# Queries, keys, gate weights and the residual turned by VectorE and strided transfers instead of TensorE, with rotation and masks at other places, in a two-block float32 transformer kernel

## What is computed

```python
def first_block(x, ...):
    z_a, z_b, z_c, z_g = split(rms_norm(x, ln1_g) @ w_in)
    u, v = split(gelu(z_a)); v = layer_norm(v)
    y_a = (u * chunked_spatial_gating(v, sg_w, sg_b)) @ w_a_out   # tril(sg_w[g]), 8 groups of 128x128
    p, g = split(z_b); c = p * sigmoid(g)
    y_b = silu(layer_norm(depthwise_conv(c, 31 taps))) @ w_b_out
    q, k, vv = split(z_c)                                        # 8 heads of 64
    q = rms_norm(q per head); k = rms_norm(k per head)
    y_c = stick_breaking_attention(q, k, vv) @ w_c_out
    x = x + (gates[0] * y_a + gates[1] * y_b + gates[2] * y_c) @ w_out
    return x + (silu(gate) * val) @ w_down                       # up-projection and 3-tap convolution
def second_block(x, ...):
    u, g_rnn, q, k, v, g_attn, m_rnn, m_attn = split(rms_norm(x) @ w_in_2)
    y_rnn  = rg_lru(depthwise_conv(u, 4 taps)) * silu(g_rnn)
    y_attn = sliding_window_attention(rope(q), rope(k), v, sinks) * silu(g_attn)
    merged = sigmoid(m_rnn) * (y_rnn @ w_rnn_out_2) + sigmoid(m_attn) * (y_attn @ w_attn_out_2)
    return rms_norm(x + merged @ w_o_2)
```

## Time and profile before

| what | value |
|---|---|
| median of three runs | 1305.08 us |
| lowest, highest | 1303.37, 1305.54 us |
| profiled execution, its own time | 1305.04 us |
| span of its profile | 1303.3 us |
| TensorE busy | 1288.0 us |
| VectorE busy | 844.4 us |
| ScalarE busy | 601.7 us |
| GpSimd busy | 86.2 us |
| DMA, mean over the span | 103 GB/s |
| mean granted TensorE clock | 0.997 |

### The profile page before, as it was taken

The page is one execution under the profiler, slowest core; times in us unless marked ns, Lnnn a source line. Parts: engine busy times, 40 slices in busy tenths (PEclk is TensorE's granted clock), DMA queues, the critical chain, the costliest instruction groups (busy, mean ns, idle before and its releaser), DMA issues.

```text
span 1303.3 us, 15597 instructions
## 1 busy us (share of the span) xinstructions
PE 1288.0 (99%) x5951; PEld 1038.5 (80%) x5951; DVE 844.4 (65%) x1128; ACT 601.7 (46%) x878; POOL 86.2 (7%) x68
## 2 busy tenths in 40 slices
PE   9999999999999999999999999999999999999998
PEld 7888777788788888888888888887877777778886
DVE  6358899899867776666675335545467878544534
ACT  6234467332354443333343224412379899544233
POOL 0000222000000300000000002100012220000000
PEclk9999999999999999999999999999999999999999
DMA  8332211422322232322223222458322122224211
GB/s 296 139 98 64 66 66 65 161 85 83 124 68 95 98 97 97 97 97 97 97 97 97 97 97 93 166 161 200 119 79 73 65 81 69 94 65 162 97 65 64
DMA packets 121129, 134.48 MB, mean 103 GB/s; under 512 B 23752, under 2 KB 101488, under 8 KB 120560
## 3 DMA queue, kind: packets, MB, share of 16 engines
q1 hardware_dynamic: 121056, 133.70, 31.6%
q10 hardware_dynamic: 16, 0.00, 0.0%
HBM read 124.78 MB, written 8.91 MB: 103 GB/s over the span
## 4 chain that ended last, share of the span: by engine, by line
PE 93%; DVE 4%; ACT 1%; issue 1%; DMA 1%; SPq 0%; ACTq 0%; DVEq 0%
PE PS L1750 91%; PE PS L1817 2%; DVE WL L1069 1%; DMA XTOK<-in_x 1%; ACT WH L625 0%; DVE QK L1171 0%; DVE CACC L1224 0%; DVE RS L1265 0%; DVE MERG L1340 0%; DVE TMPY L1336 0%; DVE VATT L1153 0%; DVE VSG L1153 0%; ACT BT L712 0%; DVE Q L1533 0%; DVE UU L1239 0%
## 5 line engine op out<-in xcount | busy, mean ns | idle before, releaser
L625 ACT ACTIVATE WH<-STAGE 128x1024 fp32r<-128x1024 f32 x214 | 225.9, 1058 | 522.0 <-PE PS L1750 515.6
L1069 DVE TENSOR_TENSOR WL<-STAGE,WH 128x1024 fp32r<-128x1024 f32 x214 | 279.5, 1308 | 190.4 <-ACT WH L625 189.7
L1750 PE MATMUL PS<-XH,WH 128*128 128x512 f32 x960 | 381.8, 398 | 2.7 <-DVE YA L1565 2.7
L1750 PE MATMUL PS<-XH,WL 128*128 128x512 f32 x960 | 374.6, 390 | 0.0
L1750 PE MATMUL PS<-XL,WH 128*128 128x512 f32 x960 | 374.5, 390 | 0.0
L1750 PEld LDWEIGHTS PS<-XH,WH 128*128 128x128 f32 x960 | 180.7, 188 | 45.2 <-issue 4.0
L1750 PEld LDWEIGHTS PS<-XL,WH 128*128 128x128 f32 x960 | 180.6, 188 | 38.7 <-issue 2.4
L1750 PEld LDWEIGHTS PS<-XH,WL 128*128 128x128 f32 x960 | 180.6, 188 | 38.2
L1750 PE MATMUL PS<-WH,XH 128*128 128x512 f32 x224 | 87.9, 392 | 0.2 <-issue 0.2
L1750 PE MATMUL PS<-WH,XL 128*128 128x512 f32 x224 | 87.2, 389 | 0.0
L1750 PE MATMUL PS<-WL,XH 128*128 128x512 f32 x224 | 87.2, 389 | 0.0
(11 more groups left out here) (295 smaller groups left out, 1812.5 us busy)
## 6 DMA issues: line engine op xcount, KB each, us to landing
STAGE<-in_w_in SPq DMA_DIRECT2D x52, 1024.0 KB, 5.0
STAGE<-in_w_up SPq DMA_DIRECT2D x22, 1024.0 KB, 5.1
STAGE<-in_w_down SPq DMA_DIRECT2D x11, 1024.0 KB, 4.9
STAGE<-in_w_out SPq DMA_DIRECT2D x4, 1024.0 KB, 5.1
STAGE<-in_w_rnn_out SPq DMA_DIRECT2D x4, 1024.0 KB, 5.3
STAGE<-in_w_attn_out SPq DMA_DIRECT2D x4, 1024.0 KB, 5.1
STAGE<-in_w_o SPq DMA_DIRECT2D x4, 1024.0 KB, 5.0
XTOK<-in_x SPq DMA_DIRECT2D x4, 512.0 KB, 7.2
```

Of the source, the lines that this page charges most:

```text
L625: act.activation(ring(WH, n), staged(n), ACT.Copy).then_inc(hi_done, 1)
L1069: dve.tensor_tensor(ring(WL, n), staged(n), ring(WH, n).bitcast(F32), ALU.subtract)\
L1750: return pe.matmul(out_, lhsT, rhs, start=start, stop=stop, skip_group_check=True)
```

## The change

It touches five places. (1) The sums, the root and the scaling of queries and keys are done for each half by itself, directly behind its drains (iterations 8 and 10), and VectorE turns the tiles in 32x32 blocks in place; SyncE's queue stores them with four strided transfers, loads them as QKT, and ScalarE applies the gain in place. (2) The gate weights are loaded with their 32x32 blocks already exchanged (four transfers, later than before), turned and masked by VectorE. (3) The residual is turned in place by VectorE in units U_G + 10 and + 11 (loop indices; X1 is dead afterwards), stored in four strided transfers and loaded as XT2; XRES, its 32 turns and ScalarE's four copies go, and the two halves of the last product swap their PSUM banks. (4) Rotation, turns and drains of the second block are spread between the splits of units 8 to 13 of stage U_G, the keys' behind the first drain of U_GA. (5) Masks stand ahead of `lo`, the gating's norm starts ahead of stage U_B's drains, the convolution's norm moves one unit later, and the fourth turn of the input stands ahead of the wait for unit 1's weights.

```diff
+            def qk_store(i):
+                for a in range(4):
+                    sp.dma_start(QKROW[i].rearrange("(b j) (t a i) -> a j t b i", j=32, a=4, i=32)[a],
+                                 QK[32 * a:32 * a + 32, i].rearrange("p t (b i) -> p t b i", i=32))...
+            def qk_load(i):
+                sp.wait_ge(qk_out[i], 64)
+                sp.dma_start(QKT[:, i], QKROW[i].rearrange("(c p) s -> p c s", p=P))...
...
+                if p == U_B // 2 - 3:
+                    for a in range(4):
+                        sp.dma_start(SGW[32 * a:32 * a + 32]..., sg_w[0].rearrange("g (b i) (a j) -> a i g b j", i=32, j=32)[a])...
+                if p == U_B // 2:
+                    sp.wait_ge(qk_turned, TT)
+                    qk_store(0)
+                if p == U_B // 2 + 1:
+                    qk_load(0)
+                    sp.wait_ge(qk_turned, 2 * TT)
+                    qk_store(1)
+                if p == U_B // 2 + 2:
+                    qk_load(1)
...
                 if p == U_G // 2 + 7:
                     sp.wait_ge(q2_turned, TT)
                     q2_store(0)
+                    sp.wait_ge(x1_turned, KD)
+                    x1_store(0)
+                    x1_store(1)
                 if p == U_G // 2 + 8:
                     q2_load(0)
+                    x1_store(2)
+                    x1_store(3)
-                if p == U_G // 2 + 4:
-                    sp.wait_ge(drained, DR_G)
-                    sp.dma_start(XSCR, X1[:].rearrange("p k s -> p (k s)")).then_inc(x1_out, 16)
-                if p == U_H // 2 + 12:
-                    sp.dma_start(XRES[:].rearrange("p k s -> p (k s)"), XSCR).then_inc(x1_in, 16)
+                if p == U_H // 2 + 15:
+                    sp.wait_ge(x1_out, 64)
+                    sp.wait_ge(unit_done, U_H + 24)
+                    sp.dma_start(XT2[:], XROW.rearrange("(t p) d -> p t d", p=P)).then_inc(xt2_in, 16)
...
             act.wait_ge(vec_ready, 3)
-            qkt_copies(0)
-            act.wait_ge(vg_var, 1)
-            act.activation(SMALL[...], SMALL[...], ACT.Sqrt).then_inc(vg_sd, 1)
+            qkt_scaled(0)
...
-            for t in range(TT):
-                act.wait_ge(x2t_t, t + 1)
-                act.activation(XT2[:, t, :], PS[...], ACT.Copy).then_inc(x2t_ready, 1)
...
+            gate_norm(0)
             for i in range(12):
                 dve.tensor_tensor(dst, PS[:, i % 2, :], RBC[:], ALU.mult).then_inc(drained, 1)
...
-                lo(U_B + i + 4)
                 if 2 <= i < 13:
                     pair_mask(i - 1)
+                lo(U_B + i + 4)
...
-                if p == 1:
+                if p == 2:
                     dve.wait_ge(c_mean, 1)
...
+                if j == 0:
+                    lo(U_G + 8)
+                    q2_rope(0)
+                    lo(U_G + 9)
+                    q2_turn(0)
+                    lo(U_G + 10)
+                    x1_turn((0, 1, 2, 3))
+                    lo(U_G + 11)
+                    x1_turn((4, 5, 6, 7))
+                if j == 1:
+                    lo(U_G + 12)
+                    q2_rope(1)
+                    lo(U_G + 13)
+                    q2_turn(1)
+                    lo(U_G + 14)
+                    lo(U_G + 15)
             for m in range(KD):
                 dve.tensor_tensor(YA[:, m, :], PS[:, m % 2, :], RBC[:], ALU.mult).then_inc(drained, 1)
                 lo(U_GA + m + 4)
+                if m == 0:
+                    rope(K2[...], KVH, 2)
+                    dve.transpose(k2, k2).then_inc(k2_turned, 1)
...
                     if t == 0:
-                        unit(n)
                         if n > U_A:
                             x_turn(3)
+                        unit(n)
...
-                if i == 0:
-                    pe.wait_ge(drained, DR_B)
-                    for j in range(2):
-                        pe.wait_ge(qk_ready, 4 * j + 4)
-                        for c in range(KW):
-                            for t in range(TT):
-                                last = tr(PS[:, bank, t * P:(t + 1) * P],
-                                          QK[:, j, t, c * P:(c + 1) * P])
-                if i == 1:
-                    pe.wait_ge(qkt_ready, 6)
-                    for q in range(2):
-                        for g in range(4):
-                            last = tr(PS[:, 6 + q, g * P:(g + 1) * P], SGW[:, 4 * q + g, :])
...
-            x_tokens(0)
-            x_tokens(1)
             for u in range(4):
-                tm_unit(U_O + u, u, 0, M2H, M2L, m2_parts, lambda t: pe.wait_ge(drained, DR_O))
-                if u < 2:
-                    x_tokens(2 + u)
-            pe.wait_ge(x2t_ready, TT)
+                tm_unit(U_O + u, u, 4, M2H, M2L, m2_parts)
+            pe.wait_ge(drained, DR_O)
```

More of the change, by code:

```diff
@@ L677, in _ @@
                 j, t = divmod(n - 4, 4)
[L678 to L686, removed]
@@ L1133, in _, with ssq, token_drain, qk_sums @@
                               tok.unsqueeze(2).broadcast_to([P, TT, P]), ALU.mult).then_inc(rt_diag, 1)
-            ssq = SMALL[:, S_QKS:S_QKS + 64]
+            def ssq(i):
+                return SMALL[:, S_QKS + 32 * i:S_QKS + 32 * i + 32]
+            def token_drain(j, t):
+                dst = (QK[:, 0, t, :], QK[:, 1, t, :], VSG[:, t, :], VATT[:, t, :])[j]
+                dve.tensor_scalar(dst, PS[:, 4 * (j % 2) + t, :], rtok(t), None, ALU.mult)\
+                   .then_inc(drained, 1)
+            def qk_sums(j, t):
+                dve.wait_ge(qk_sq, 4 * j + t + 1)
+                dve.tensor_reduce(SMALL[:, S_QKS + 8 * (4 * j + t):S_QKS + 8 * (4 * j + t) + 8],
+                                  TG1[:].rearrange("p (h d) -> p h d", d=DH), AX.X, ALU.add)\
+                   .then_inc(qk_red, 1)
+            def qk_norm(i):
+                dve.wait_ge(qk_rt, i + 1)
+                link(dve.reciprocal(ssq(i), ssq(i)))
+                for tt in range(TT):
+                    c = S_QKS + 8 * (4 * i + tt)
+                    v = QK[:, i, tt, :].rearrange("p (h d) -> p h d", d=DH)
+                    dve.tensor_tensor(v, v, SMALL[:, c:c + 8].unsqueeze(2)
+                                      .broadcast_to([P, HEADS, DH]), ALU.mult).then_inc(qk_ready, 1)
+                for tt in range(TT):
+                    dve.wait_ge(qk_ready, 4 * i + tt + 1)
+                    dve.transpose(QK[:, i, tt, :], QK[:, i, tt, :]).then_inc(qk_turned, 1)
             for n in range(U_A, U_B + 4):
@@ L1174, in _ @@
-                if n == U_B + 3:
-                    dve.wait_ge(bc_in, 16 * 12)
-                    for tt in range(TT):
+                if n >= 4 and t == 0:
+                    dve.wait_ge(unit_done, U_A + 4 * j + 4)
+                if 4 <= n < 8:
+                    token_drain(0, t)
+                    qk_sums(0, t)
+                if n in (8, 9):
+                    for tt in (2 * t, 2 * t + 1):
+                        token_drain(1, tt)
+                        qk_sums(1, tt)
+                if n in (12, 13):
+                    token_drain(2, 2 * t)
+                    token_drain(2, 2 * t + 1)
@@ L1178, in _ @@
+                if n in (U_B - 2, U_B - 1):
+                    for tt in (2 * t - 4, 2 * t - 3):
                         dve.wait_ge(vg_ready, tt + 1)
@@ L2225, in _ @@
             pe.wait_ge(pv_read, 16)
-            pe.wait_ge(x1_in, 16)
-            def x_tokens(t):
-                if t >= 2:
-                    pe.wait_ge(x2t_ready, t - 1)
-                for k in range(KD):
-                    last = tr(PS[:, 4 + 2 * (t % 2) + k // 4, k % 4 * P:(k % 4 + 1) * P],
-                              XRES[:, k, t * P:(t + 1) * P])
-                last.then_inc(x2t_t, 1)
             def m2_parts(k):
```

196 lines of the change are left out of this document (102 added, 94 removed).

## The result

The changed kernel takes **1289.42 us** (median of 4 runs, 1289.10 to 1289.76), the kernel before, on the same chip, 1304.22 (median of 4, 1303.37 to 1305.54): a ratio of 0.9884, interval 0.9872 to 0.9897.

What follows compares the result with a forecast made beforehand. TensorE, busy 1288.0 of 1303.3 us, was taken as the bound. Removed turns 8.17 plus waits 5.9 less a new wait 0.6 gave 13.5 us off 1305.04: 1291.5 us, range 1289.8 to 1296.5 (8 in 10).

Steps and rivals of the forecast that it cites:

- order of rotation, wait for YA: Second block: spreading VectorE's rotation and turns between splits removes TensorE's wait for the YA drain, 2.7 us.
- residual's turns: Removing the residual's (XRES) 32 turns from TensorE: 1.66 us for the first 16, 0.79 for each of two groups; 3.24 us.
- mask, norm, fourth turn: TensorE's waits go: BT and AT by the earlier mask 1.6, TG by the later norm 1.2, input turn 0.4 us.
- turns of QK and SGW, new wait: First attention: removed turns give 3.95 and 0.98 us; TensorE newly waits 0.6 us for QKT before the first scores.
- I take the full 2.7: Second block, wait for YA: all 2.7 us listed come off, nothing as the low end.
- the split of the convolution's result: One unit nearer its use at unit U_C + 32: left at zero cost, 2 us if it comes late.
- a wait under 1 us: Sign at the first scores, near 112 to 113 us: TensorE's wait named after QKT stays under 1 us.
- the keys' load near 107: Sign in the first attention: the keys' load lands near 107 us, put at 107.2.
- 9.1 us after the first: SyncE's queue, first attention: keys' load can follow 9.1 us after their first store, as in the second block.
- Back pressure from VectorE: Rival, around 200 to 210 us: VectorE sets the pace, 6.5 us return as waits, 1298.0 us; chance 0.13.
- The late round trip: Rival, keys' stores and load: half as long again (8 us), TensorE waits 6.4 us, 1297.3 us; chance 0.13.
- the weights of units 20 and 21 late: Rival "slower than before": queue waits delay these weights past TensorE's need at 118 us; total over 1305 us; chance 0.03.

Runs made afterwards that it cites:

- experiment 1: Kernel before with only the second block's rotation and turns in the new order, the keys' part behind the first YA drain: 1300.44 us, ratio 0.9969.
- experiment 10: Kernel before with the second block's new order and the residual turned by VectorE, stored and loaded as XT2: 1296.78 us.
- experiment 11: Changed kernel without the first attention's queries, keys and gate weights parts, nor the gate's earlier norm and ScalarE's new order there: 1293.38 us.
- experiment 2: Kernel before with 24 unread turns of the identity on TensorE ahead of the wait for YA: 1303.54 us, ratio 0.9991.
- experiment 3: Changed kernel with six waits of different lengths put into TensorE's stream in stages U_G and U_GA: 1307.13 us, one run.
- experiment 6: Changed kernel with the convolution's norm back one unit earlier, as before: 1290.81 us.
- experiment 5: Changed kernel with the split ahead of the pair mask again: 1291.01 us.
- experiment 4: Kernel before with only the pair mask moved ahead of the split in stages U_B and U_C: 1303.08 us, ratio 0.9986.

## Why the prediction was right and where it was wrong

**The sum by its parts.** By experiments 1, 10 and 11 and the change itself, from 1304.95 down (the medians come from several chips, on which before took 1304.85 to 1305.03, so by an estimate each part is good to 0.2 us):

```
part                              predicted          measured
order of rotation, wait for YA    2.7                4.5
residual's turns                  3.24               3.66
mask, norm, fourth turn           1.6 + 1.2 + 0.4    3.40
turns of QK and SGW, new wait     4.93 - 0.6         3.96
sum                               13.5               15.5
```

**The step that failed** is "I take the full 2.7" for YA. The mechanism was right, the wait is gone and nothing came in its place; the term was mis-sized. A wait of TensorE was priced by its idle time, with that as the upper bound ("the full 2.7; nothing as the low end"). In the trace of before it also has the stretch at half clock, 1.7 us, and experiments 1, 2 and 3 show that an idle time of this length is followed by one: 4.5 without the wait, 1.4 back with work in it, 1.6 for each of three waits made for the purpose. The window rows behind the prediction lie at 160 and 200 us; at the largest wait the PEclk column has 0.58. With 2.68 + 0.15 (the gap of 3.06 less one normal distance of 0.23 is 2.83) + 1.7 = 4.5 the sum would have been 15.3 and the forecast 1289.7.

**Residual's turns.** Right in kind and 0.4 too small. The two later groups were taken as 0.79 each, and the unit behind a group of turns also begins with a slower start (0.48 for the first matmul at 1251.50, 0.39 without turns before it).

**Mask, norm, fourth turn.** 3.2 forecast, 3.40 measured. The norm gave 1.4 instead of 1.2, a slow start again; the mask 1.6 to 1.9 instead of 1.6; the fourth turn is left with 0.1 to 0.4. That the split of the convolution's result would not come late held: no wait stands there after.

**QK, SGW and the new wait.** The turns came off as read; the new wait is 1.4 instead of 0.6. It moves between executions: the profiles of experiments 6, 5 and 3, where this part is the same, have 1.1, 0.9 and 0.8. Two of the prediction's own signs were missed here: a wait under 1 us, and the keys' load near 107. TensorE's own arrival was right (111.9 against a forecast of 112.0), the queries' turns end at 74.6 (75.2) and the keys' at 87.7 (88.5 to 89). The keys' stores were issued from 89.9 (90.7). Late was "9.1 us after the first": the load followed 14.7 us after the first store, where the row it was taken from, in the second block, has 9.1. During those stores of before (865.4 to 874.6 us) the DMA share is 0.78, against 0.98 from the keys' first store to their load in the change (89.9 to 104.5). The load took 6.1 instead of 7.4, so the keys landed at 110.66 instead of 107.2, and ScalarE, forecast to be the last at 112.6, began its keys' gains 1.4 us after it was free. The range for this term, 0 to 4, held it.

**The rivals.** Back pressure from VectorE did not appear: in the changed kernel it is idle for 2.2 us of the window from 160 to 165 us (busy 2.82 of 5.00), and experiment 5 shows no other wait. The late round trip did begin, 3.5 us of the 8 that it was given, and cost 0.8. Nothing made the weights of units 20 and 21 late. The range fell short on its lower side because none of its bounds let a removed wait give back more than its record: it reached 5.0 us up, towards the rivals, and 1.7 down.

## What to carry to other kernels

Price a wait of the bounding TensorE by the distance between the matmuls around it and by the granted clock and the distances behind it, not by the list of waits alone: here 2.7 us listed were 4.5 us of time. If such a wait can't be removed, work that nobody reads in it can give back what the clock costs; if it can, moving the work of the late engine behind the drain is better, and here that was a matter of a few lines. And before a store or a load is moved earlier, read the DMA share of the stretch: at 93% an earlier start was worth nothing, while four operations less behind the load were worth 1.0 us.

## What the runs showed of the hardware

The two groups of runs of before fit the clock. Of its 39 executions beside the experiments, 13 took 1303.2 to 1303.6 us, each with a mean granted clock of 0.999, and 26 took 1304.7 to 1305.7, each with 0.997 or 0.998; the groups are some 1.6 us apart, the cost of one stretch. The kernel of experiment 4, which keeps the wait, has both groups; those of experiments 1 and 2, without the idle time, have one each. No profile of a run of before in the lower group was taken, so that its stretch is missing there is inferred, from the time above all. The mean clock is the weaker sign, since it also takes in the end of the program, where TensorE is done (0.52 in before from 1300 to 1303 us) and the runs of experiment 2 have 0.998 to 1.0. By this inference the idle time of 2.68 us is followed by half clock in 26 of 39 executions. In the profiles here none of 1.61 us or less is followed by it, and the one of 2.07 us is, in its single execution.

In the first attention the strided stores of 128-byte runs cost between 7.6 and 10.3 us to issue for 1 MB, by what ran beside them, where the same kind had taken 5.69 in another place of the same program.
